# Opening of a two-layer transformer kernel: a gain row spread by TensorE, first halves of two tiles turned first, and zero products

## What is computed

```python
def rms_norm(x, gain):
    xf = x.astype(jnp.float32)
    y = xf * lax.rsqrt(jnp.mean(xf * xf, axis=-1, keepdims=True) + RMS_EPS)
    return (y * gain.astype(jnp.float32)).astype(x.dtype)
...
        h = rms_norm(x, pre_mix_norm[l])
        proj = h @ w_in[l]
        q, k, v_a, u, v_s = jnp.split(
            proj, [ATTN_WIDTH, 2 * ATTN_WIDTH, 3 * ATTN_WIDTH, 3 * ATTN_WIDTH + SGU_WIDTH], axis=-1)
```

## Time and profile before

| | us |
|---|---|
| median of 3 runs | 1794.17 |
| lowest, highest | 1792.36, 1796.28 |
| the profiled execution, its own time | 1793.85 |
| its span on the core | 1792.0 |

### The profile page before, as it was taken

How to read it: one execution, slowest core, us unless ns; L and a number is a source line. 1 busy time by engine, 2 the same in 40 slices (tenths; PEclk the granted TensorE clock), 3 DMA queues, 4 the chain that set the end, 5 groups by cost and what they waited for, 6 DMA issues and landing times.

```text
span 1792.0 us, 24688 instructions
## 1 busy us (share of the span) xinstructions
PE 1761.5 (98%) x9544; PEld 1442.0 (80%) x9544; DVE 1158.6 (65%) x1804; ACT 848.1 (47%) x1604; POOL 366.7 (20%) x433
## 2 busy tenths in 40 slices
PE   7999999999999999999999999999999999999998
PEld 7767898888888877878878787777788998888877
DVE  6655647348336787887778856677646457574838
ACT  5446534234334564564645634545435445343536
POOL 1503011100000046363453630000110012112112
PEclk9999999999999999999999999999999999999999
DMA  7221383944322444443444443234444247849482
GB/s 249 82 60 62 96 241 88 275 123 126 110 94 70 155 140 139 129 143 116 144 131 133 135 169 138 82 118 125 134 142 152 69 146 174 242 101 271 111 204 71
DMA packets 146052, 246.06 MB, mean 137 GB/s; under 512 B 27712, under 2 KB 59904, under 8 KB 145040
## 3 DMA queue, kind: packets, MB, share of 16 engines
q1 hardware_dynamic: 118976, 166.70, 29.5%
q0 software_dynamic: 26096, 75.30, 16.5%
q10 hardware_dynamic: 864, 2.49, 0.4%
HBM read 229.64 MB, written 14.81 MB: 136 GB/s over the span
## 4 chain that ended last, share of the span: by engine, by line
PE 83%; DVE 11%; ACT 2%; DMA 2%; issue 1%; POOL 0%; SPq 0%; DVEq 0%; ACTq 0%
PE m L2220 14%; PE m L2222 14%; PE m L2221 14%; PE m L2231 5%; PE m L2233 5%; PE m L2232 5%; PE s L2385 3%; PE m L2330 3%; PE m L2331 3%; PE m L2332 3%; DVE lo L1457 2%; DMA raw<-in_w_up_dram 2%; PE m L2357 2%; PE s L2381 1%; PE m L2359 1%; PE m L2358 1%
## 5 line engine op out<-in xcount | busy, mean ns | idle before, releaser
L2220 PE MATMUL m<-hH,hi 128*128 128x512 f32 (+1 forms) x1392 | 530.4, 381 | 3.7 <-DVE hL L1489 1.6
L2222 PE MATMUL m<-hH,lo 128*128 128x512 f32 (+1 forms) x1392 | 509.7, 366 | 0.0
L2221 PE MATMUL m<-hL,hi 128*128 128x512 f32 (+1 forms) x1392 | 509.0, 366 | 0.0
L1457 DVE TENSOR_TENSOR lo<-raw,hi 128x1024 fp32r<-128x1024 f32 (+1 forms) x253 | 318.4, 1268 | 172.9 <-ACT hi L975 172.4
L975 ACT ACTIVATE hi<-raw 128x1024 fp32r<-128x1024 f32 (+1 forms) x253 | 262.2, 1051 | 210.4 <-DMA raw<-in_w_up_dram 108.7
L2220 PEld LDWEIGHTS m<-hH,hi 128*128 128x128 f32 x1392 | 263.3, 189 | 48.3 <-DVE hL L1489 2.5
L2222 PEld LDWEIGHTS m<-hH,lo 128*128 128x128 f32 x1392 | 263.1, 189 | 43.6
L2221 PEld LDWEIGHTS m<-hL,hi 128*128 128x128 f32 x1392 | 263.7, 189 | 38.8
L2231 PE MATMUL m<-hi,hH 128*128 128x512 f32 (+1 forms) x320 | 132.9, 415 | 2.2 <-DVE lo L1457 2.2
L2233 PE MATMUL m<-hi,hL 128*128 128x512 f32 (+1 forms) x320 | 122.0, 381 | 0.0
L2232 PE MATMUL m<-lo,hH 128*128 128x512 f32 (+1 forms) x320 | 121.8, 381 | 0.0
(11 more groups left out here) (359 smaller groups left out, 3131.2 us busy)
## 6 DMA issues: line engine op xcount, KB each, us to landing
raw<-in_w_in_dram SPq DMA_DIRECT2D x72, 512.0 KB, 3.7
wq<-in_w_down_dram POOLq DMA_DIRECT2D x40, 512.0 KB, 10.6
hn<-scr_cs_dram POOLq DMA_DIRECT2D x32, 512.0 KB, 4.3
raw<-in_w_up_dram SPq DMA_DIRECT2D x32, 512.0 KB, 5.6
wq<-in_w_down_dram SPq DMA_DIRECT2D x24, 512.0 KB, 7.5
raw<-in_w_gate_dram SPq DMA_DIRECT2D x44, 256.0 KB, 3.5
raw<-in_w_up_dram SPq DMA_DIRECT2D x44, 256.0 KB, 4.4
raw<-in_w_in_dram SPq DMA_DIRECT2D x33, 256.0 KB, 3.1
```

The source lines that it names most:

```text
L1457: e.tensor_tensor(d, r, h.bitcast(F32), ALU.subtract).then_inc(s_lo, 1)
L2220: e.matmul(bank, wh[:, kk, c], h[:, k, q], start=k == 0, stop=False)
L2221: e.matmul(bank, wh[:, kk, c], l[:, k, q], start=False, stop=False)
L2222: x = e.matmul(bank, wl[:, kk, c], h[:, k, q], start=False, stop=k == kt - 1)
```

## The change

- The gain is loaded as one row of 1024 elements into partition 0 of `G[0]`, on SyncE's queue between tile 0 and the identity. Two plain fp32 products with a row of ones (`ONE`, on partition 0, filled by GpSimd) spread it over 128 partitions into the PSUM banks `side[2]` and `side[3]`. `norm_scale` of tiles 0 to 3 reads the gain there.
- The half tiles are taken in another order: first halves of tiles 0 and 1, then their second halves, then tiles 2 and 3 alike (`half_of`, `turn_of`). Turns use `side[0]` and `side[1]` only. Two turns stand ahead of block q, the other six lie in its slots 1, 2, 5, 6, 8 and 9. Block q starts when two rests are made.
- VectorE splits unit 0 ahead of the two rests. ScalarE splits unit 1 behind round 1, and unit 2 and the squares of tiles 2 and 3 behind round 3.
- VectorE fills `LO[5]`, free at that time, with zeros. TensorE multiplies it with itself into `main[0]`, 6 times before the spread, 6 before turn 0, 2 between the turns and 8 before block q.

```diff
+def half_of(i):
+    return (2 * (i // 4) + i % 2, i % 4 // 2) if i < 8 else (i // 2, i % 2)
+def turn_of(n, b):
+    return 4 * (n // 2) + 2 * b + n % 2 if n < 4 else 2 * n + b
...
-    N_S0.append(-1), N_S1.append(-1), N_HN.append(-1), N_TR.extend([(-1, -1), (-1, -1), (2, 3), (4, 5)][t])
+    N_S0.append(-1), N_S1.append(-1), N_HN.append(-1), N_TR.extend([(-1, -1), (1, 2), (5, 6), (8, 9)][t])
...
+        s_zero = sem("s_zero")
+        s_gbc, GBC_FROM = s_zero, 2
+        def turned(i):
+            return side[i % (2 if i < 8 else 4)]
+        ONE = PT[1][0:1, 0:128]
...
             e.dma_start(X[:, 0, :], A["x"][0, 0:128, :]).then_inc(s_x[0], 16)
+            e.dma_start(G[0][0:1, :], A["pre_mix_norm"]).then_inc(s_gain[0], 16)
             e.dma_start(CST[:, 0:128], A["consts"][:, 0:128]).then_inc(s_id, 16)
...
-            e.dma_start(G[0][:, :], A["pre_mix_norm"][0].partition_broadcast(128)).then_inc(s_gain[0], 16)
...
             split_weights(0)
             norm_round(0)
             norm_round(1)
+            split_weights(1)
             norm_round(2)
             norm_round(3)
-            split_weights(1)
             norm_squares(2, 1)
             split_weights(2)
             norm_squares(3, 1)
             split_weights(3)
+            norm_round(4)
+            norm_round(5)
...
+            e.memset(LO[5][:, 0, :].bitcast(F32), 0.0).then_inc(s_zero, 1)
...
                 if n >= 2:
-                    o.wait_ge(s_ntr, 2 * n - 2)
+                    o.wait_ge(s_ntr, max(turn_of(n - 2, h) for h in halves) + 1)
...
-                for h in range(2):
+                for h in halves:
                     k = slice(512 * h, 512 * h + 512)
+                    if n < 4:
+                        o.wait_ge(s_gbc, GBC_FROM + h + 1)
+                    gain = side[2 + h][:, :] if n < 4 else G[i % 2][:, k]
...
-            norm_scale(0)
+            norm_scale(0, (0,))
             o.wait_ge(s_sq1, 1)
-            norm_scale(1)
+            norm_scale(1, (0,))
+            split_weights(0)
             norm_rest(0)
             norm_rest(1)
-            split_weights(0)
+            norm_scale(0, (1,))
+            norm_scale(1, (1,))
+            split_weights(1)
             norm_rest(2)
             norm_rest(3)
-            split_weights(1)
-            norm_scale(2)
             split_weights(2)
-            norm_scale(3)
+            norm_scale(2, (0,))
+            norm_scale(3, (0,))
             split_weights(3)
+            norm_rest(4)
+            norm_rest(5)
+            norm_scale(2, (1,))
+            norm_scale(3, (1,))
...
+            e.memset(ONE, 1.0).then_inc(s_zero, 1)
...
-                o.wait_ge(s_nlo, 2 * n0 + 4 * h + (3 if u < 2 else 4))
+                o.wait_ge(s_nlo, 2 * n0 + 4 * h + ((2 if b.name == "q" else 3) if u < 2 else 4))
...
+            def zeros(n):
+                for _ in range(n):
+                    e.matmul(main[0][:, :], LO[5][:, 0, 0:128], LO[5][:, 0, :], start=True, stop=True)
...
-            for i in range(4):
-                norm_turn(i)
+            o.wait_ge(s_zero, 2)
+            zeros(6)
+            o.wait_ge(s_gain[0], 16)
+            for h in range(2):
+                e.matmul(side[2 + h][:, :], ONE, G[0][0:1, 512 * h:512 * h + 512], start=True, stop=True).then_inc(s_gbc, 1)
+                read["side", 2 + h] = (s_hn, 8)
+            zeros(6)
+            norm_turn(0)
+            zeros(2)
+            norm_turn(1)
+            zeros(8)
```

More of the change, by code:

```diff
@@ L998, in norm_round @@
             def norm_round(i):
-                n, b = i // 2, i % 2
+                n, b = half_of(i)
                 o.wait_ge(s_ntr, i + 1)
@@ L1008, in norm_round @@
                 dst = (mH if 12 <= n < 14 else hH)[:, 4 * b:4 * b + 4, 128 * t:128 * t + 128]
-                e.activation(dst, side[i % 4][:, :].rearrange("p (k t) -> p k t", k=4), ACT.Copy).then_inc(s_nhi, 1)
+                e.activation(dst, turned(i)[:, :].rearrange("p (k t) -> p k t", k=4), ACT.Copy).then_inc(s_nhi, 1)
             def evacuate(b, i):
@@ L1398, in scalar_program @@
                 for i in TR_AT.get(g - 1, ()):
[L1399 removed]
+                    if i >= 6:
                         norm_round(i)
@@ L1457, in split_weights, with norm_scale @@
                 e.tensor_tensor(d, r, h.bitcast(F32), ALU.subtract).then_inc(s_lo, 1)
-            def norm_scale(n):
+            def norm_scale(n, halves=(0, 1)):
                 t = n % 4 if n < 12 else n - 12 if n < 14 else (n - 14) % 4
@@ L1463, in norm_scale @@
                 r = st(ST_N[n] + 2)
-                if n < 18:
+                if n < 18 and 0 in halves:
                     o.wait_ge(s_nrs, n + 1)
                     e.reciprocal(r, r).then_inc(*o.own())
-                else:
+                elif n >= 18:
                     o.wait_ge(s_nrp, n - 17)
-                o.wait_ge(s_gain[i % 2], GAIN_LANDED[i])
+                if n >= 4:
+                    o.wait_ge(s_gain[i % 2], GAIN_LANDED[i])
                 if n >= 2:
-                    o.wait_ge(s_ntr, 2 * n - 2)
+                    o.wait_ge(s_ntr, max(turn_of(n - 2, h) for h in halves) + 1)
                 if 8 <= n < 12:
@@ L1477, in norm_scale @@
                 o.settle()
-                for h in range(2):
+                for h in halves:
                     k = slice(512 * h, 512 * h + 512)
-                    e.scalar_tensor_tensor(out=HN[n % 2][:, k], in0=src[:, k], scalar=r, in1=G[i % 2][:, k], op0=ALU.mult, op1=ALU.mult).then_inc(s_hn, 1)
+                    if n < 4:
+                        o.wait_ge(s_gbc, GBC_FROM + h + 1)
+                    gain = side[2 + h][:, :] if n < 4 else G[i % 2][:, k]
+                    e.scalar_tensor_tensor(out=HN[n % 2][:, k], in0=src[:, k], scalar=r, in1=gain, op0=ALU.mult, op1=ALU.mult).then_inc(s_hn, 1)
             def norm_rest(i):
-                n, b = i // 2, i % 2
+                n, b = half_of(i)
                 o.wait_ge(s_nhi, i + 1)
@@ L1488, in norm_rest @@
                 c = slice(128 * t, 128 * t + 128)
-                e.tensor_tensor(l[:, k, c], side[i % 4][:, :].rearrange("p (k t) -> p k t", k=4), h[:, k, c].bitcast(F32), ALU.subtract).then_inc(s_nlo, 1)
+                e.tensor_tensor(l[:, k, c], turned(i)[:, :].rearrange("p (k t) -> p k t", k=4), h[:, k, c].bitcast(F32), ALU.subtract).then_inc(s_nlo, 1)
             def output_gain(b, i):
@@ L1976, in vector_program @@
                 for i in TR_AT.get(g - 1, ()):
-                    if i >= 4:
+                    if i >= 6:
                         norm_rest(i)
@@ L2387, in norm_turn @@
             def norm_turn(i):
-                n, b = i // 2, i % 2
-                claim("side", i % 4)
+                n, b = half_of(i)
+                bank = i % (2 if i < 8 else 4)
+                claim("side", bank)
                 o.wait_ge(s_id, 16)
@@ L2393, in norm_turn @@
                     c = 512 * b + 128 * k
-                    x = transpose(side[i % 4][:, 128 * k:128 * k + 128], HN[n % 2][:, c:c + 128])
+                    x = transpose(turned(i)[:, 128 * k:128 * k + 128], HN[n % 2][:, c:c + 128])
                 x.then_inc(s_ntr, 1)
-                read["side", i % 4] = (s_nlo, i + 1)
+                read["side", bank] = (s_nlo, i + 1)
+            def zeros(n):
+                for _ in range(n):
+                    e.matmul(main[0][:, :], LO[5][:, 0, 0:128], LO[5][:, 0, :], start=True, stop=True)
             def mixture(g):
```

## The result

Over 20 runs each, the changed kernel took 1797.04 us in the median and the kernel before 1793.01: a ratio of 1.0021, 95% interval 1.0016 to 1.0027. It is slower, by 4.0 us. The forecast was 0.8 us and "no change"; the time lies inside the range of 1791.8 to 1797.6, near its upper end. The range hung on the median of three runs, 1794.17, which 20 runs put at 1793.01; the change itself, 4.0 against 0.8, was missed by 3.2. The profiled execution has a span of 1795.1 us against 1792.0.

What follows compares the result with a forecast made beforehand. TensorE's work list, busy 98%, was taken as the bound. Start 0.7 us earlier, 1.4 of slow clock saved, turns 0.9, waits 1.6 and 0.5 put slot 12 0.8 later: 1795.0, range 1791.8 to 1797.6.

Steps and rivals of the forecast that it cites:

- yardstick: Block q as 16 slots of 1.44 us plus turns of 0.44; slot 12's start is compared, 33.9 before the change.
- The wait at slot 4: In block q, TensorE waits 1.6 us for unit 2, which comes late in ScalarE's list.
- the one at slot 12: Late in block q, TensorE waits 0.5 us for the rest of turn 7, behind VectorE's angles.
- the two turns: Two more turns lie inside block q than before, adding 0.9 us.
- the start of block q: First product of block q at 12.7 us, 0.7 earlier, at 2.4 GHz, decided by the zero products.
- the first, the spread: Opening, TensorE: two plain fp32 products of 512 columns at 0.86 us each, ending at 7.5.
- the second, the clock: Opening, TensorE: clock rises at 8.9 us, 3.2 after 5.7, during the six zeros behind the spread.
- rival (3): Opening: plain fp32 products stream columns four times; block q starts at 13.8, slot 12 1.9 us later, 1796.1; chance 0.05.
- rival (2): Opening: clock rises only at 12.0, zeros end at 14.3; slot 12 2.4 us later, 1796.6; chance 0.13.
- Nothing behind the first block is gated by something that the change leaves where it is: After the first block: whatever that block loses or wins is carried to the end, nothing added there.
- Rival (4): Opening: clock never up before real products; block q starts at 16.0, slot 12 5.5 us later, 1799.7; chance 0.04.
- from a start later than 15.5: Block q's start past which the clock staying down until real products decides; 14.1 if first real products run slow.

Runs made afterwards that it cites:

- e4: Changed kernel with ScalarE doing squares of tile 2 ahead of round 2 and unit 2 ahead of round 3: 1796.72 us, 1.0014 to the kernel before.
- e1: Changed kernel with the gain loaded to all partitions by DMA again, no spread, order and zeros kept: 1796.24 us, 1.0015 to the kernel before.
- e2: Changed kernel without all 22 zero products, spread and order kept: 1801.11 us, 1.0039 to the kernel before.
- e3: Changed kernel with only its new order of half tiles: gain by DMA, no spread, no zeros: 1799.15 us, 1.0029 to the kernel before.
- e9: New order alone, gain by DMA, no zeros, with ScalarE's squares of tile 2 and unit 2 moved ahead of rounds 2 and 3: 1795.03 us, 1.0013 to before.
- e8: Changed kernel with 0.5 in place of 0 in the 22 filling products: 1797.84 us, 1.0026 to the kernel before.
- e5: Kernel before with zero products added in TensorE's idle time, 15 ahead of its four turns and 5 behind: 1792.62 us, 0.9999 to the kernel before.
- e10: New order, ScalarE's moved steps, gain row and spread kept, 6 zeros ahead of the spread and 5 behind turn 1: 1793.46 us, 0.9999 to before.
- e6: New order, gain by DMA, ScalarE's moved steps, 15 zeros ahead of turn 0 and 5 behind turn 1: 1791.58 us, 0.9993 to the kernel before.
- e11: Repeat of the kernel with new order, gain by DMA, ScalarE's moved steps, 15 and 5 zeros: 1792.76 us, 0.9996 to the kernel before.

## Why the prediction was right, and where it wasn't

**Right in its yardstick and its inner waits.** The wait at slot 4 was 1.49 us against 1.6, the one at slot 12 0.3 against 0.5, the two turns 0.9, and the first block at full speed from its first product. From q to k it is 27.7 us in the profile against 27.8 by the forecast's sum (40.5 - 12.7).

**Wrong in the start of block q**, 16.49 against 12.7, and this is all of the difference in k (44.20 against 40.5). That the time still lay in the range was in part luck: the median that it started from was 1.2 us too high. Two steps failed. Taken along TensorE's list, the first, the spread, cost 2.0 us of the 3.8 (3.70 for 1.7), and the second, the clock, 1.7 in the zeros and turns behind it; 0.1 is the gain's later landing.

*The spread's price.* "0.21 us each" for eight plain fp32 products came from a row that counts records. The program has four instructions of L2461 there, and the trace two records for each (x8); the changed kernel's two spreads are four records in the same way. So one of 256 columns takes 0.41 us, and the spread of two times 512 took 3.7 us slow and 1.9 fast, not 1.7 and 0.9. It was rival (3), which the prediction had 1.1 us above its forecast and gave a chance of 0.05. The Trainium skill, page "FP8 and Floating Point Precision", section "TensorE Precision Notes", has four passes for true fp32; the trace agrees, with 0.96 us for 512 columns at the fast clock against 0.23 for a product of block k. I had let a misread row overrule it.

*The clock.* "If the clock rises 3.2 us after 5.7" was taken from a single rise. It came at 14.4 in the changed kernel's profile, at about 4.5 in e4's, fell again in e1 and e4, and came 5 us after the first product in e2 and e3. That was rival (2), by its own sum 1.6 us above the forecast. Zero products at some 0.45 in strict order ahead of the turns then cost twice what they cost at 0.23.

**Wrong in what a wait costs.** I priced the wait at slot 4 at its length. In e2 and e3, where it was 2.3 and 2.9 us long, the clock fell behind it, and e9 without it is 4.1 us faster than e3. In the changed kernel's own profile, and in that of e8, it was 1.5 long and the clock stayed up, so how much of the median comes from this is not shown. GpSimd's step, which made the wait longer in e2 and e3, stands in no sum of the prediction.

**Wrong in one smaller step.** "Nothing behind the first block is gated by something that the change leaves where it is" doesn't hold near the end: the two loads of `w_up` gate there, and in the profiled executions they took back 1.0 us.

**The sign.** The forecast put 0.87 on no change beyond 0.2%; the measured 0.21% sits on that line. Rival (4), the only one that I called slower, isn't what happened: real products began on a fast clock. It took rivals (2) and (3) together: 1.6 and 1.1 on top of the 0.8 by their own sums, 3.5 in all, and 4.5 in the profile, since the clock rose at 14.4 and not at 12.0 as rival (2) counts, and four passes at the slow clock also push the zeros behind them back. I had given the two separate chances and no joint one. The bound "from a start later than 15.5" did hold: the start was 16.49.

The gain of the opening that the edit was to bring did exist in part: the order alone starts q 1.4 us earlier (e3), zeros in idle time save the slow products (e5). The wait on unit 2, the spread ahead of the turns and zeros that stand in the way took more than that.

## What to carry to other kernels

Count instructions in the program before dividing a row of the trace by its count: the plain fp32 products here left two records each. Filler work that keeps TensorE's clock up belongs where TensorE is idle by the profile, sized so that it also fits at half the clock; put in front of work that is ready, it costs its own length, and at the slow clock about twice as much (0.45 us against 0.23 here). When work is moved from before a block into it, follow the other engines' lists: a unit that used to be ready with 4 us to spare waited here behind a step that had become late, and where GpSimd made that wait longer the clock fell behind it.

## What the runs showed of the hardware

- The granted clock column reads 1.00 in every profile up to the clock's first rise, although the spacing there is that of 1.2 GHz (0.45 us for a zero product ahead of 14.4 in the changed kernel, 0.24 behind). Later falls are shown (0.50 in 24:27 of e3).
- The clock's rise lay at other places in executions whose TensorE had the same list up to there: at about 4.5 us in e4, at 14.4 in the changed kernel. That may be part of the spread of single runs, 1790.4 to 1796.9 for the kernel before; no run here separates it.
- With the clock up at its beginning, the spread of one row was followed by a fall in e4 although TensorE had no idle time there (it had stood idle for 1.26 us just before); with six zeros ahead of it the clock was not up at its end in e10 either. Full-size zero products kept it up in e5 and e6 through idle stretches of 1.9 and 1.2 us, but not through 1.9 us in e1. What tells these apart stays open.
- VectorE steps that read two SBUF tiles and started while GpSimd's step on the tile `MIX` ran took 2.59 us for 1.22 (e3), 2.03 for 1.22 (e2) and 2.62 for 0.75 (e1, e9). The first two ended 1.1 us behind GpSimd's, the others 0.5 to 0.6. A split that started later in it took 1.72 in e4 and 1.58 in e10, again ending 1.1 behind. Steps with one tile in PSUM kept their times meanwhile (0.75 for a scaling in e4, 0.69 for a rest in e8). In e6 and e11 the split had started first: it took its 1.22, and GpSimd's step 3.2 and 3.3 us instead of 2.4.
